# Two-layer hybrid diffusion step on one core: modulation groups, weight splits and layer 1's first norm in another order

## What is computed

```python
for l in range(2):
    mod_l, mod_c = silu(c) @ w_ada[l] + b_ada[l], silu(c_ctx) @ w_ada[l] + b_ada[l]   # 6 x 1024 each
    hl = modulate(rmsnorm(xl, norm1_g[l]), mod_l[0], mod_l[1])
    hc = modulate(rmsnorm(xc, norm1_g[l]), mod_c[0], mod_c[1])
    hy_l, pool_l, cq_l, ckv_l, kpe_l = split(hl @ w_in[l])     # and the same for hc
    k_c, v_c = mla_kv(ckv_c, kpe_c, ...); k_l, v_l = mla_kv(ckv_l, kpe_l, ...)
    att_l = attention(mla_q(cq_l, ...), [k_c, k_l], [v_c, v_l])
    y = concat(hyena_mix(hy_l, filter(l)), pool_mix(pool_l), att_l) @ w_out[l]
    xl = xl + mod_l[2] * y             # layer 0: the same for the context stream
    xl = xl + mod_l[5] * channel_mix(modulate(rmsnorm(xl, norm2_g[l]), mod_l[3], mod_l[4]))
return rmsnorm(xl, final_g)
```

## Time and profile before

| | us |
|---|---|
| median of 3 runs | 1709.87 (1708.15 to 1710.27) |
| the profiled execution | 1708.7 |
| its span, first to last instruction | 1706.8 |
| around the span | 1.9 |
| PE busy, of the span | 1618.1 (95%) |
| DVE busy | 1294.3 (76%) |
| ACT busy | 891.7 (52%) |

### The profile page before, as it was taken

How to read it: one execution, slowest core, us unless ns; L and a number is a source line. 1 busy time by engine, 2 the same in 40 slices (tenths; PEclk the granted TensorE clock), 3 DMA queues, 4 the chain that set the end, 5 groups by cost and what they waited for, 6 DMA issues and landing times.

```text
span 1706.8 us, 19495 instructions
## 1 busy us (share of the span) xinstructions
PE 1618.1 (95%) x7452; PEld 1273.2 (75%) x7452; DVE 1294.3 (76%) x1733; ACT 891.7 (52%) x1019; POOL 14.1 (1%) x30
## 2 busy tenths in 40 slices
PE   5998999899999999798789999999999999999996
PEld 2885668678788887685487778787887878788774
DVE  3844573797787756854668998898988889898897
ACT  3322372322222222434557777777777776777764
POOL 1000000000000000000000000000000000000000
PEclk9999999899999999899889999999999999999999
DMA  9226421444445553132137999999999999999992
GB/s 391 81 78 236 147 80 50 172 182 169 173 172 200 220 199 122 34 114 94 61 149 285 352 343 337 346 356 359 351 334 362 347 355 346 343 347 370 344 347 107
DMA packets 55971, 403.43 MB, mean 236 GB/s; under 512 B 6416, under 2 KB 6448, under 8 KB 8768
## 3 DMA queue, kind: packets, MB, share of 16 engines
q1 hardware_dynamic: 53712, 387.47, 60.5%
q0 software_dynamic: 2160, 14.63, 2.3%
HBM read 401.03 MB, written 1.05 MB: 236 GB/s over the span
## 4 chain that ended last, share of the span: by engine, by line
PE 76%; DVE 15%; ACT 5%; issue 3%; DMA 1%; SPq 0%; DVEq 0%; ACTq 0%
PE PS L439 20%; PE PS L441 20%; PE PS L440 20%; DVE w_lo L2254 6%; ACT w_hi L1480 3%; PE PS L737 2%; DVE arena L1616 1%; DVE w_lo L1603 1%; PE PS L993 1%; PE PS L762 1%; PE PS L749 1%; DMA arena<-in_ada 1%; PE PS L698 1%; PE PS L449 1%; PE PS L704 1%
## 5 line engine op out<-in xcount | busy, mean ns | idle before, releaser
L2254 DVE TENSOR_TENSOR w_lo<-arena,w_hi 128x2048 fp32r<-128x2048 f32 x132 | 301.7, 2290 | 43.9 <-ACT w_hi L1480 43.9
L2254 DVE TENSOR_TENSOR w_lo<-raw,w_hi 128x2048 fp32r<-128x2048 f32 x129 | 295.0, 2291 | 32.8 <-ACT w_hi L1480 32.4
L1480 ACT CAST w_hi<-arena 128x2048 fp32r<-128x2048 f32 x132 | 251.6, 1909 | 47.0 <-PE PS L441 47.0
L1480 ACT CAST w_hi<-raw 128x2048 fp32r<-128x2048 f32 x129 | 246.9, 1916 | 44.4 <-PE PS L441 44.4
L439 PE MATMUL PS<-hT_hi,w_hi 128*128 128x512 f32 (+1 forms) x576 | 217.6, 378 | 12.2 <-DVE hT_lo L1751 10.6
L440 PE MATMUL PS<-hT_lo,w_hi 128*128 128x512 f32 (+1 forms) x576 | 214.6, 373 | 0.0
L441 PE MATMUL PS<-hT_hi,w_lo 128*128 128x512 f32 (+1 forms) x576 | 214.4, 372 | 0.0
L439 PE MATMUL PS<-w_hi,hT_hi 128*128 128x512 f32 (+1 forms) x448 | 178.3, 398 | 0.3 <-DVE w_lo L2254 0.3
L441 PE MATMUL PS<-w_hi,hT_lo 128*128 128x512 f32 (+1 forms) x448 | 174.6, 390 | 0.0
L440 PE MATMUL PS<-w_lo,hT_hi 128*128 128x512 f32 (+1 forms) x448 | 173.5, 387 | 0.0
L1603 DVE TENSOR_TENSOR w_lo<-raw,w_hi 128x2048 fp32r<-128x2048 f32 (+1 forms) x54 | 122.3, 2266 | 34.8 <-ACT w_hi L1109 34.6
(11 more groups left out here) (320 smaller groups left out, 2520.2 us busy)
## 6 DMA issues: line engine op xcount, KB each, us to landing
raw<-in_moe SPq DMA_DIRECT2D x132, 1024.0 KB, 6.9
arena<-in_moe SPq DMA_DIRECT2D x132, 1024.0 KB, 6.9
raw<-in_ffn SPq DMA_DIRECT2D x33, 1024.0 KB, 4.8
raw<-in_dot SPq DMA_DIRECT2D x28, 1024.0 KB, 4.8
raw<-in_ada SPq DMA_DIRECT2D x17, 1024.0 KB, 7.3
raw<-in_out SPq DMA_DIRECT2D x8, 1024.0 KB, 4.8
raw<-in_inb SPq DMA_DIRECT2D x8, 960.0 KB, 4.8
raw<-in_ina SPq DMA_DIRECT2D x5, 1024.0 KB, 5.4
```

The source lines that it names most:

```text
L1480: nc.scalar.copy(w_hi[:, x_slot(j), :], x_raw(n)).then_inc(x_hi, 1)
L2254: v.tensor_tensor(w_lo[:, x_slot(j), :], x_raw(NGR * (i % 2) + j), w_hi[:, x_slot(j), :].bitcast(F32), ALU.subtract).then_inc(x_lo, 1)
```

## The change

In layer 0, groups 5 to 9 go elsewhere: 5 after the transposed latents, 6 between keys and values, 7 between values and queries, 8 between query pairs 3 and 4, 9 after the queries. `bias_mod` and `save_row` follow, and keys and values take banks in turn. The splits of `out 0` to `out 2` on ACT come behind row 7; on DVE `out 0` comes behind the copies of the values. In layer 1, filter products 8 to 10 leave the feed-forward and stand around sum and spread. The first norm does the latent stream; the context stream's norm comes after the split of `inb 2`, on ACT ahead of the copies of `B 0`; `B 1` takes latent tiles first. `out 0` is split on ACT ahead of the rope keys' copies; `out 1` and `out 2` move behind the queries (ACT: in attention and after; DVE: in `project_out`).

```diff
 def filter_beside(b):
     n = b // 3 + 2
-    return n if b % 3 == 0 and 3 <= n <= 10 else None
+    return n if b % 3 == 0 and 3 <= n <= 7 else None
...
+        def own_tiles(l, b):
+            return (0, 1, 2, 3) if l == 0 else (2, 3, 0, 1) if b else (2, 3)
...
                 for pr in range(4):
-                    o = bank(f"k {l} {pr}", pr)
+                    o = bank(f"k {l} {pr}")
...
                 for t in range(NT):
-                    o = bank(f"v {l} {t}", 4 + t)
+                    o = bank(f"v {l} {t}")
...
                 if l:
+                    filters(1, 8)
                     norm_sum(l, 1, (0, 1))
+                    filters(1, 9)
                     norm_spread(l, 1, (0, 1))
+                    filters(1, 10)
                     state["next"] = 0
...
@@ ScalarE, project_in
                 else:
-                    eng.wait_ge(dve_done, after(f"t 1 1 {KD - 1} 0"))
+                    upto(gindex[("inb", 1, 2, 0)])
+                    norm(1, 1, (0,))
...
@@ ScalarE, latents
+                if l == 0:
+                    save_row(0, 5)
+                else:
+                    upto(gindex[("out", 1, 0, 0)])
...
-                if l == 0:
-                    save_row(0, 7)
-                upto(gindex[("out", l, 0, 0)])
...
-                upto(gindex[("out", l, 2, 0)])
                 if l == 0:
+                    save_row(0, 6)
+                    save_row(0, 7)
+                    upto(gindex[("out", 0, 2, 0)])
                     save_row(0, 8)
+                    save_row(0, 9)
...
@@ VectorE, latents
-                    if pair in (1, 3):
-                        upto(gindex[("out", l, 1 + pair // 2, 0)])
+                    if l == 0 and pair in (1, 3):
+                        upto(gindex[("out", 0, 1 + pair // 2, 0)])
+                    if l == 0 and pair == 3:
+                        bias_mod(0, 7)
...
@@ VectorE, project_out
-                upto(ahead(g, 2))
+                upto(ahead(g, 1 if l else 2))
...
+                    if l and k == 1:
+                        upto(ahead(g, 2))
```

More of the change, by code:

```diff
@@ L485, in filters @@
             def filters(l, n):
-                b = 7 if l else None
+                b = {8: 0, 9: 3, 10: 2}.get(n, 7) if l else None
                 if n == 3:
@@ L570, in project_in @@
                 for b in range(2):
-                    ts = tiles_of(streams) if b == 0 else range(NT)
-                    os = {t: bank(f"B {l} {b} {t}") for t in ts}
+                    ts = own_tiles(l, b)
+                    os = {t: bank(f"B {l} {b} {t}", (6, 0, 1, 2, 3, 4)[2 * b + ts.index(t)] if l else None) for t in ts}
+                    if l:
+                        state["next"] = 5
                     for half in range(2):
@@ L576, in project_in @@
                         for t in ts:
+                            if l and t < 2:
+                                eng.wait_ge(dve_done, after(f"hT 1 1 {4 * half + 3} 0"))
                             for k in range(4):
@@ L687, in latents @@
                 if l == 0:
[L688 to L691 removed]
+                    turn(0, 4)
+                    plain(5)
                 eng.wait_ge(*loaded[f"kv {l}"])
@@ L700, in latents @@
                     did(f"k {l} {pr}")
+                if l == 0:
+                    turn(0, 5)
+                    plain(6)
                 for t in range(NT):
-                    o = bank(f"v {l} {t}", 4 + t)
+                    o = bank(f"v {l} {t}")
                     for k in range(KKV):
@@ L706, in latents @@
                     did(f"v {l} {t}")
+                if l == 0:
+                    turn(0, 6)
+                    plain(7)
                 for k in range(KQ):
@@ L719, in latents @@
                     did(f"q {l} {pair}")
+                    if l == 0 and pair == 3:
+                        turn(0, 7)
+                        plain(8)
                 if l == 0:
-                    turn(0, 7)
-                    plain(8)
+                    turn(0, 8)
+                    plain(9)
             def attention(l, streams):
@@ L1203, in norm @@
                         act(hT_hi[:, k, q], tb[:, k, q], ACT.Identity, bias=shift).then_inc(act_done, 1)
-                        did(f"hThi {l} {w} {k}")
-                    if k == 3 and (l, w) == (1, 1):
-                        upto(gindex[("ina", 1, 1, 0)])
+                        did(f"hThi {l} {w} {k} {s}")
             def project_in(l, streams):
@@ L1235, in project_in @@
                         filters(0, 9)
-                    for t in (tiles_of(streams) if b == 0 else range(NT)):
+                    for t in own_tiles(l, b):
                         eng.wait_ge(pe_done, after(f"B {l} {b} {t}"))
@@ L1368, in attention @@
                         save_turned(first[n] + half)
-                    if l == 0 and n == 0:
-                        save_row(0, 9)
                     if n % 2 and n >= 3:
                         mix_high((n - 3) // 2)
+                    if l and n == 5:
+                        upto(gindex[("out", 1, 1, 0)])
                 mix_high(len(heads) // 2 - 1)
@@ L1548, in _ @@
                     deviation(1, 1, (0, 1))
-                norm(l, 1, (0, 1))
+                if l:
+                    filters(1, 8)
+                norm(l, 1, streams)
+                if l:
+                    filters(1, 9)
+                    filters(1, 10)
                 project_in(l, streams)
@@ L1746, in norm @@
                     if k >= 0:
-                        eng.wait_ge(act_done, after(f"hThi {l} {w} {k}"))
+                        eng.wait_ge(act_done, after(f"hThi {l} {w} {k} {streams[-1]}"))
                         for s in streams:
@@ L1893, in latents @@
                 sp = span(streams)
-                if l == 0:
-                    bias_mod(0, 6)
-                upto(gindex[("out", l, 0, 0)])
+                if l:
+                    upto(gindex[("out", 1, 0, 0)])
                 for t in range(NT):
@@ L1900, in latents @@
                     did(f"Vs {l}", f"read v {l} {t}")
+                if l == 0:
+                    bias_mod(0, 6)
+                    upto(gindex[("out", 0, 0, 0)])
                 heads = attention_plan(streams)[0]
```

32 lines of the change are left out of this document (8 added, 24 removed).

## The result

| | before | after |
|---|---|---|
| median, us | 1709.01 (4 runs, 1707.86 to 1710.27) | 1698.65 (4 runs, 1697.93 to 1700.34) |
| ratio after to before, 95% interval | | 0.9944, 0.9931 to 0.9957 |
| span of the profiled execution | 1706.8 | 1696.8 |

The changed kernel is 10.4 us faster, 0.4 to 0.7%. The forecast was 14.3 us less than before; the range held the time. Two terms of the sum make up nearly the whole difference: the feed-forward gave 1.7 us less than forecast, and layer 1's attention, forecast at 0, costs 2.7 us.

What follows compares the result with a forecast made beforehand. PE, busy 95% of the span, was taken as the bound. Terms -4.3 - 4 + 0.9 - 9.9 + 3 = -14.3 us from 1708.7 gave 1694.4, forecast as median 1695.6, with 1690 to 1700 from bounds and a range of 1687 to 1704.

Steps and rivals of the forecast that it cites:

- Feed-forward: Filter products 8, 9 and 10 leave a stage where PE is full, so their whole time is saved: -4.3 us.
- Head of layer 1 and context norm: Filter products fill gaps and a one-stream norm shortens the head, -4; PE waits for `inb 3` in the context norm, +0.9.
- Keys to scores: Layer 1: keys and values run without bank waits, two splits leave DVE's queries, first maximum comes earlier: -9.9 us.
- Attention of layer 1: The moved `out 1` cast (1.9 us) fits ACT's 2.1 us to spare per pair of heads: 0 us.
- Layer 0: Queries start 8.1 us earlier, but bank waits, a 3.1 us gap and the low clock behind it cost more: +3 us.
- +7: Upper bound for layer 0: the clock also falls at group 8, slows pairs 4 and 5, and lasts into attention.
- The rivals: Layer 0 pays fully: 1701, 0.15; no clock fall: 1689, 0.10; filter products bring nothing: 1700, 0.05; slower: 1717, 0.02.
- The third: Filter products bring nothing because another engine sets the feed-forward's pace; 4.3 us stay, giving 1700; chance 0.05.

Runs made afterwards that it cites:

- experiment 6: Changed kernel with DVE's split in layer 0's feed-forward passes behind the third chunk's additions instead of the second's; 1697.62 us, ratio 0.9929 to before.
- experiment 3: Changed kernel with filter products 8, 9 and 10 back in the feed-forward; 1702.32 us, ratio 0.9958 to before.
- Experiment 9: Changed kernel with the context stream back in layer 1's first norm, both streams chunk by chunk; 1701.41 us, ratio 0.9962 to before.
- Experiments 10: Changed kernel with layer 1's `out 1` and `out 2` splits back among DVE's queries, their ACT casts behind the key copies; 1702.85 us, ratio 0.9966 to before.
- 11: Changed kernel with layer 1's keys in fixed PSUM banks 0 to 3 and values in 4 to 7; 1703.06 us, ratio 0.9968 to before.
- experiment 1: Kernel before with only layer 0's part of the change, the new order of modulation groups; 1712.01 us, ratio 1.0022 to before.
- Experiment 4: Changed kernel with layer 1's `out 1` cast on ACT directly behind the key copies instead of in the last pair of heads; 1696.92 us, ratio 0.9928 to before.
- experiment 5: Changed kernel with layer 0's last modulation group in other PSUM banks (turn 4 instead of 7, product 5 instead of 6); 1692.07 us, ratio 0.9902 to before.
- experiment 2: Changed kernel with layer 0's mixing in the order of before, so layer 1's part alone; 1694.96 us, ratio 0.9918 to before.
- 8: Changed kernel with free banks for the last modulation group, later feed-forward split, product 9 ahead of the sum and `out 1` cast ahead of scores; 1688.24 us, ratio 0.9880.
- Experiment 12: The kernel with four edits together, plus layer 0's groups 8 and 9 back at their old places, banks 3 to 6; 1683.10 us, ratio 0.9851 to before.

## Why the prediction was right, and where its sum was off

**Feed-forward, -4.3 forecast, -2.6 measured.** The step that failed is "PE is full there, so this is -4.3 in that stage". The products were sized rightly. PE in before around product 9, the matmul ahead of the earlier trace rows and the second one behind:

```profile
568.62 0.39 PE L441 MATMUL PS<-hT_hi,w_lo 128*128 128x512 f32 x1
...
570.81 0.39 PE L440 MATMUL PS<-h_lo,w_hi 128*128 128x512 f32 x1
```

Between these starts pass 2.19 us, and 0.46 in after, where the product is gone: 1.73 us, as forecast. What had it wrong is "full": nothing waited while the products were there, but each product had covered a late bank. In three passes PE now waits for additions that stand on DVE behind a split of 2.28 us; a wait shows as 0.35 us and costs 0.6 (experiment 6). 4.3 less three times 0.6 is 2.5, measured 2.57. Before had two such waits, at 644.90 and 678.47, where no product stood ahead of them; the forecast looked at 500 to 600 only. With the products put back (experiment 3) the three waits go; with the split moved (experiment 6) all five go.

**Head of layer 1 and context norm, -3.1 forecast, -5.2 measured,** 1.0 of which is the shorter wait ahead of the keys, which the prediction counted with the keys. The mechanism was right: chunks 0.8 us apart, spread late by 1.45 us at a low clock (2.5 was allowed), product 10 hidden, wait of 0.62 us for the split of `inb 3` (0.9 forecast). Experiment 9 gives the order of the streams 4.8 us, experiment 3 the products 3.9 us in all, 1.4 of it at the head. 4.8 and 1.4 are more than the 4.2 that head and context norm gained, so the two overlap; by how much was not measured.

**Keys to scores, -9.9 forecast, -9.5 measured** (8.5 within and 1.0 ahead). Experiments 10 and 11 split it: 4.65 for the two splits (4.6 forecast), 3.2 for the banks (5.1 forecast with the keys' two waits). The other 1.7 us are luck: the fall of the clock in the keys of before, which stood in the forecast's 5.1 too and which experiment 1 does not have. The gap ahead of the fourth score was 4.20 us, forecast 3.7.

**Attention of layer 1, 0 forecast, +2.7 measured.** The failed step is "ACT has 2.1 us to spare for each pair of heads". That is true in the middle, where work is queued ahead. The cast lands in the last pair, where no later pair is in flight, and there 1.9 us on ACT turn into two new waits of PE (0.54 and 0.50 us; before had the third too, 0.93) and a fall of the clock. Experiment 4 shows it: 3.2 us. Some 2.4 of them are the fall, which came in five of eight executions, so this term is 0.5 or 2.9 us by chance.

**Layer 0, +3 forecast, +3.05 measured.** The mechanism was right. Waits of 0.87, 0.71 and 3.19 us were forecast as 0.8, 0.7 and 3.1; the wait of 0.4 for the granule did not show (its 4.8 us in the earlier trace rows belong to the output weights; the page has 7.3 us for `raw<-in_ada`, and even so nothing waited). The low clock came once, behind the longest, and for about 6.8 us; where it lasted 3.4 us the stretch was 1.3 us shorter, so the close match of the size is partly luck. The Trainium skill, "TensorE: Matmul & The Clock Gate", section "A second HAM failure mode: psum-queue depth-cycling", says that short idles from cycling through PSUM banks make the clock swing between its levels. The prediction put +7 on that. Here the two short bank waits left the granted clock at 1.00 up to the wait of 3.19 us; one fall came behind one long wait, as in the row at 164. What the prediction missed is that this one wait had a cure in two numbers, worth 6.4 us in that stretch.

**The rivals.** None of the four took place. The third came nearest in size: 1.7 of the feed-forward's 4.3 us did stay away, but by three single waits for a bank that DVE reads late, not because another engine sets the pace of the whole stage.

**The sum.** Feed-forward 1.7 short, attention 2.7 short, head, keys and layer 0 together 0.7 better, 0.5 of small shifts: 14.3 - 1.7 - 2.7 + 0.7 - 0.5 = 10.1, the difference of the two spans. That head and context norm gained 1.1 us more than forecast made up for part of the two errors, and that is luck too.

## What to carry to other kernels

Before taking work off a full engine, look at what that work covers: compare a pass with it and a pass without it in the trace of before. Whatever is moved "where an engine has slack" must be placed by the slack of that very place; at the end of a pipelined loop there is none. In experiment 5 other bank numbers alone removed a wait, so after every reordering look up who reads each awaited bank last and choose one that was read long ago. And price a wait by starts with it and without it, not by the idle time shown.

## What the runs showed of the hardware

The granted clock did not answer to the same idle time in the same way. Behind the wait of 3.19 us in layer 0 the low stretch was about 3.4 us in four executions and 6.8 in five (64.9 to 65.0 and 66.2 to 66.3 us for the stretch). Behind 2.17 us ahead of the sum at the head of layer 1 it was about 3.4 us in after, 6.8 in experiment 6, and missing in experiment 2. Behind the 1.61 us for layer 0's first exponential the clock fell in experiment 5 and not in 8. Behind the cast in the last pair it fell in five traces of eight. This moves a span by 1.1 to 2.4 us at each such place, as much as most of the single edits here, so one profiled execution can't price a gap that is near the edge. Stretches without a fall repeat: keys to fourth score took 31.11 to 31.12 us in ten traces. The one long wait in this stretch, 4.20 us, stands at its end, and the clock falls only in it or behind it. Experiment 12 has no low clock from 150 to 222.
